# Two transformer blocks on one core: where the pooling chunks, the memory split and the row scaling run in the attention steps

## The reference, cut to what matters

```
h = rmsnorm(x); proj = h @ w_in            # 1024 -> 1888 columns, split in: conv pair, MLA q/kv/rope, diff q/k/v, pool
ya = silu(layernorm(causal_dwconv(a * sigmoid(g)))) @ pw + pw_b       # 31 taps, 256 channels
yb = mla(...)                              # 4 heads, causal softmax over 512 keys
yc = diff_attention(...)                   # 4 heads, two softmax maps each: p = a0 - lam * a1
yd = multiscale_pool(ud)                   # window means of 2, 4, 8, 16 tokens minus the token, times pool_w, pool_scale
x += concat(ya, yb, yc, yd) @ w_out
x += memory_cross_attention(rmsnorm(x), mem)   # k = m @ wk, v = m @ wv, 256 memory tokens
x += conv_glu_ffn(rmsnorm(x))              # 1024 -> 5632 -> 2816 -> 1024
```

## Time and profile before

| | |
|---|---|
| median of 3 runs | 1760.46 us (1758.02 to 1761.1) |
| profiled execution | 1760.47 us, span 1758.6 us |
| busy, share of the span | PE 93%, PE weight load 71%, DVE 63%, ACT 40%, POOL 18% |
| mean granted TensorE clock | 0.962 of full speed |
| scores of step 0, layer 0 and layer 1 | at 196.62 and 1019.22 us |
| end of the last step's work, layer 0 and layer 1 | at about 393.1 and 1214.1 us |

### The profile page before, as it was taken

One profiled execution on the slowest core, in us unless ns is written; L12 is line 12 of the kernel. 1 busy time (PEld: TensorE's weight loads), 2 busy tenths in 40 slices (PEclk: granted clock), 3 DMA queues, 4 the chain that ended last, 5 costly groups with the idle time before them and its releaser, 6 DMA issues. The chain is left out here.

```text
span 1758.6 us, 21905 instructions
## 1 busy us (share of the span) xinstructions
PE 1630.3 (93%) x7472; PEld 1253.1 (71%) x7472; DVE 1108.6 (63%) x1592; ACT 698.8 (40%) x1074; POOL 308.2 (18%) x216
## 2 busy tenths in 40 slices
PE   6889979889999999999998988898999999999996
PEld 3567566568767888888876666666877788888874
DVE  8967785655345764764764867665444675575576
ACT  3132345753244432432442243764343442342343
POOL 6510174522002000000020027551101100000002
PEclk9989899999999999999998998999999999999998
DMA  3242122313202232323324212322211222322323
GB/s 134 52 148 84 49 72 96 102 51 100 84 24 84 96 95 96 97 96 96 95 82 138 75 48 61 109 97 72 91 54 60 84 96 96 96 95 96 96 84 107
DMA packets 46206, 153.38 MB, mean 87 GB/s; under 512 B 5808, under 2 KB 6064, under 8 KB 45232
## 3 DMA queue, kind: packets, MB, share of 16 engines
q1 hardware_dynamic: 46128, 152.34, 26.8%
HBM read 144.97 MB, written 7.34 MB: 87 GB/s over the span
## 5 line engine op out<-in xcount | busy, mean ns | idle before, releaser
L695 ACT ACTIVATE wh<-raw 128x1024 fp32r<-128x1024 f32 x246 | 260.4, 1059 | 660.9 <-PE psum L1249 660.9
L1247 PE MATMUL psum<-a_hi,wh 128*128 128x512 f32 x1072 | 426.1, 397 | 7.9 <-DVE wl L937 7.5
L1249 PE MATMUL psum<-a_hi,wl 128*128 128x512 f32 x1072 | 420.0, 392 | 0.0
L1248 PE MATMUL psum<-a_lo,wh 128*128 128x512 f32 x1072 | 420.0, 392 | 0.0
L937 DVE TENSOR_TENSOR wl<-raw,wh 128x1024 fp32r<-128x1024 f32 x234 | 288.6, 1234 | 193.4 <-ACT wh L695 193.2
L1247 PE MATMUL psum<-b_hi,wh 128*128 128x512 f32 x608 | 240.8, 396 | 10.6 <-DVE wl L937 6.1
L1247 PEld LDWEIGHTS psum<-a_hi,wh 128*128 128x128 f32 x1072 | 203.0, 189 | 57.6 <-DVE wl L937 11.5
L1248 PE MATMUL psum<-b_lo,wh 128*128 128x512 f32 x608 | 237.4, 390 | 0.0
L1249 PE MATMUL psum<-b_hi,wl 128*128 128x512 f32 x608 | 237.4, 390 | 0.0
L1248 PEld LDWEIGHTS psum<-a_lo,wh 128*128 128x128 f32 x1072 | 203.2, 190 | 44.9 <-issue 2.9
L1249 PEld LDWEIGHTS psum<-a_hi,wl 128*128 128x128 f32 x1072 | 202.9, 189 | 42.5
(11 more groups left out here) (214 smaller groups left out, 2188.3 us busy)
## 6 DMA issues: line engine op xcount, KB each, us to landing
raw<-in_w_main SPq DMA_DIRECT2D x106, 512.0 KB, 3.5
raw<-in_w_up SPq DMA_DIRECT2D x88, 512.0 KB, 3.5
raw<-in_w_down SPq DMA_DIRECT2D x32, 512.0 KB, 3.5
raw<-in_w_last SPq DMA_DIRECT2D x16, 384.0 KB, 2.9
bias_scratch<-stage SPq DMA_DIRECT2D x64, 64.0 KB, 1.6
bias<-bias_scratch SPq DMA_DIRECT2D x16, 256.0 KB, 3.9
raw<-in_w_first SPq DMA_DIRECT2D x6, 512.0 KB, 3.5
sw<-in_small SPq DMA_DIRECT2D x2, 1152.0 KB, 6.9
```

The source lines that it names most:

```text
L695: act.activation(wh[:, b].rearrange("p k m -> p (k m)")[:, 0:width], raw[:, b, 0:width], ACT.Copy).then_inc(w_hi, 1)
L1247: pe.matmul(out_ap, wh[:, b, k, :], his[:, k, :], start=(begin and i == 0), stop=False)
L1248: pe.matmul(out_ap, wh[:, b, k, :], los[:, k, :], start=False, stop=False)
L1249: last = pe.matmul(out_ap, wl[:, b, k, :], his[:, k, :], start=False, stop=(end and i == len(tiles) - 1))
```

## The change

What it does, by parts:

1. The pool chunks 13 and 14 of w_in are taken right behind chunk 6 (`IN_ORDER`), so the windows on GpSimd are built before the step loop; `pool0`, `pool1` run in steps 1 and 3. Twelve chunks, not eleven, run before the loop.
2. The memory is split tile by tile in step 2, each tile as soon as the last projection chunk has used the tile of x beneath it (`a_used`); memh and meml of a tile lie together over one tile of `a_hi`. The memory chunks start in step 3. `vc` is transposed and evicted in steps 6 and 8, in the other PSUM bank.
3. VectorE scales the rows itself: one `tensor_scalar` (128x512) behind the inverse for an MLA map; for a differential one a `tensor_scalar` on the second map and the existing combination with the inverse of the first. `wgt` and GpSimd's multiplications go.
4. GpSimd makes the lower parts of chunks 15 to 32 (before: 25 to 30).
5. Steps are moved: ln_mean 10 to 11, ln_var 14 to 15, silu 19 to 21, pw 22, 26 to 23, 25, vx 20, 24 to 18, 22; the first pair of each group of four one step later; taps 30 instead of 34 in the loop; the inverses behind the norms no longer free a PSUM bank, ScalarE's root does.

The diff, cut:

```diff
-CHUNK_AT = {**{t: 11 + t for t in range(4)}, **{t: 10 + t for t in range(5, 13)},
-            **{t: N_WV + i for i, t in enumerate((16, 18, 20, 22, 24, 27, 30, 33))}}
-POOL_LO = {15: 25, 17: 26, 19: 27, 21: 28, 23: 29, 26: 30}
+IN_ORDER = [0, 1, 2, 3, 4, 5, 6, 13, 14, 7, 8, 9, 10, 11, 12]
+CHUNK_AT = {t: 12 + i for i, t in enumerate((0, 1, 2, 3, 4, 5, 6, 7, 9, 11, 13, 15, 17, 19, 21, 23, 26, 29, 32))}
+VX_AT = {18: 0, 22: 1, 28: 2, 36: 3}
+POOL_LO = range(N_WK, N_OUT + 2)
+def pair_step(n):
+    return 2 * n + 5 + int(n % 4 == 0)
...
# GpSimd
-                    for u in range(32):
...
-                        pool.tensor_scalar(e, e, rec[:, m:m + 1], None, ALU.mult).then_inc(scaled_in, 1)
-                        if u in (3, 5):
-                            window_sums(u // 2 - 1)
-                        if u in (4, 6):
-                            window_differences(u // 2 - 2)
-                        if u in POOL_LO:
-                            lower(POOL_LO[u])
+                    for i in range(2):
+                        window_sums(i)
+                        window_differences(i)
+                    for n in POOL_LO:
+                        lower(n)
...
# ScalarE
-                        if t == 4:
+                        if t == 2:
                             act.wait_ge(memf_in, 16)
-                            act.wait_ge(g_full, N_WK)
                             for k in range(KT):
+                                if k < KT - 1:
+                                    act.wait_ge(a_used, k + 1)
+                                else:
+                                    act.wait_ge(g_full, N_WK)
                                 act.activation(memh[:, k, :], memf[:, k, :], ACT.Copy,
                                                scale=v("g_mem", k)).then_inc(m_hi, 1)
...
# VectorE
-                    for n in range(11):
+                    for n in range(12):
...
-                            convolve({8: 0, 9: 1, 10: 4}.get(n, 3))
+                            convolve({8: 0, 9: 2, 11: 4}.get(n, 3))
...
+                            dve.wait_ge(rec_in, m + 1)
+                            dve.tensor_scalar(e, e, rec[:, m:m + 1], None, ALU.mult).then_inc(scaled_in, 1)
...
-                            step(dve.scalar_tensor_tensor(wgt[:, u:u + 1], rec[:, k + 1:k + 2], lam[:, 4:5],
-                                                          sums[:, k:k + 1], ALU.mult, ALU.mult))
-                            dve.scalar_tensor_tensor(e0, e1, wgt[:, u:u + 1], e0, ALU.mult, ALU.add).then_inc(p_ready, 1)
-                        if t < 4:
+                            step(dve.tensor_scalar(e1, e1, rec[:, k + 1:k + 2], lam[:, 4:5], ALU.mult, ALU.mult))
+                            dve.scalar_tensor_tensor(e0, e0, rec[:, k:k + 1], e1, ALU.mult,
+                                                     ALU.add).then_inc(scaled_in, 1)
+                        if t < 2:
                             convolve(4)
-                        elif t > 4:
+                        elif t > 2:
                             convolve(3)
...
# TensorE
+                    gemm(11, 1, a_hi, a_lo, free="in")
...
-                        if t == 10:
+                        if t == 11:
                             pe.wait_ge(acc_done, 2)
                             product("ln_mean", (ones, acc[:, 0, :]), (ones, acc[:, 1, :]))
...
-                        if t in (20, 24, 28, 36):
-                            g = {20: 0, 24: 1, 28: 2, 36: 3}[t]
+                        if t in VX_AT:
+                            g = VX_AT[t]
                             pe.wait_ge(g_act, 8 + 2 * g + 2)
```

More of the change, by code:

```diff
@@ L79 @@
 SW_UQ0, SW_UQ1, SW_K, SW_V, SW_PW, SW_POOL, NSW = 0, 512, 1024, 1280, 1536, 2048, 2304
-V_USES = ([("stat_mix", "dve"), ("stat_q", "dve"), ("stat_kv", "dve"), ("kr", "act"), ("uq0", "dve"),
+V_USES = ([("stat_mix", "root"), ("stat_q", "root"), ("stat_kv", "root"), ("kr", "act"), ("uq0", "dve"),
            ("uq1", "dve"), ("uq2", "dve"), ("uq3", "dve")] + [(f"kn{h}", "act") for h in range(4)] +
[L85 to L91, removed]
+          [("vm0", "act"), ("vm1", "act"), ("pool0", "dve"), ("pool1", "dve"), ("vc0", "act"), ("vc1", "act"),
+           ("ln_mean", "dve"), ("mla0", "dve"), ("ln_var", "root"), ("vx0", "act"), ("mla1", "dve"), ("vx1", "act"),
+           ("pw0", "dve"), ("pw1", "dve"), ("diff0", "act"), ("vx2", "act"), ("sub0", "root"), ("diff1", "act"),
+           ("vx3", "act"), ("sub1", "root"), ("stat_xa", "root")] +
+          [(f"xo{i}", "dve") for i in range(8)] + [("stat_ffn", "root")])
+Y_ORDER = {6: "pool0", 7: "pool1", 2: "mla0", 3: "mla1", 0: "pw0", 1: "pw1", 4: "diff0", 5: "diff1"}
 Y_TILES = list(Y_ORDER)
@@ L559, in _ @@
                     sp.dma_start(vec[:], vecs[layer]).then_inc(vec_in, 16)
-                    loads_of(2, 2, w_main, src_base=2)
+                    for n in (2, 3):
+                        load(n, n % 2, w_main[layer, n])
                     sp.dma_start(sw[:], small[layer]).then_inc(sw_in, 16)
                     sp.dma_start(memf[:], mem_norm).then_inc(memf_in, 16)
-                    loads_of(4, 12, w_main, src_base=4)
-                    loads_of(16, 10, w_main, src_base=16)
+                    for n in range(4, N_WK):
+                        load(n, n % 2, w_main[layer, IN_ORDER[n]])
+                    loads_of(N_WK, 10, w_main, src_base=N_WK)
                     def load_bias(u):
@@ L725, in _ @@
                         act.activation(sqx[:, i, :], sqx[:, i, :], ACT.Sigmoid).then_inc(gate_out, 1)
-                    for n in range(3, 11):
+                    for n in range(3, 12):
                         hi(n + 2)
@@ L954, in inverse @@
                         if cols.stop == S:
-                            ins.then_inc(v_dve, 1)
-                            own_v(name)
+                            step(ins)
                     def scaled(n, dst, b=None):
@@ L1234, in _, with gemm @@
                 def _(pe):
-                    def gemm(n, b, his, los, tokens=S, free=None, tiles=range(KT), ready=None, begin=True, end=True):
+                    def gemm(n, b, his, los, tokens=S, free=None, tiles=range(KT), ready=None, begin=True, end=True, used=None):
                         if begin:
@@ L1250, in gemm @@
                                              stop=(end and i == len(tiles) - 1))
+                            if used and i < len(tiles) - 1:
+                                last.then_inc(used, 1)
                         if end:
@@ L1268, in bank @@
                             before, owner = V_USES[V_AT[V_BEFORE[name]]]
-                            pe.wait_ge(v_dve if owner == "dve" else v_act, V_FREED[owner].index(before) + 1)
+                            freed = {"dve": v_dve, "act": v_act, "root": root}[owner]
+                            pe.wait_ge(freed, V_FREED[owner].index(before) + 1)
                         return V[V_BANK[name]]
```

171 lines of the change are left out of this document (75 added, 96 removed).

## The result

The changed kernel takes 1739.68 us (median of 4 runs, 1737.64 to 1742.63) against 1760.59 for the kernel before on the same chip (4 runs, 1758.02 to 1761.1): 0.9885 of it, 95% interval 0.9868 to 0.9903. It is 20.9 us faster; 9.5 were forecast. The direction and the range held, the size did not: it is more than twice the forecast. The changed kernel was timed in the first comparison only; where others are compared with it, it stands at 0.9881, the ratio of its two medians (by the estimate of 0.9885 each such difference shifts by 0.7 us). 0.001 is 1.76 us, and the difference of two ratios is known to about 0.002, some 4 us.

The account below looks back on a forecast made before the run. TensorE was taken as the bound, busy most of the time at partly reduced clock, with VectorE just behind. Layer 0's terms summed to 191.1 against 196.5 us (-5.4), layer 1 -3.8: 1760.5 to 1751 us, range 1728 to 1771.

Parts of the forecast that it names:

- Steps 0 to 2: First three loop steps: three projection chunks, not four, plus pool0's product; 19.5 us per layer forecast.
- the memory split: Step 2 into step 3: only the last tile left at chunk 14's end; gap of 5.18 us becomes 0.8 to 1.2.
- ln_mean to step 16: Loop stretch with chunks 21 to 23, no pool product and no gap; 26.0 us forecast against 31.7 before.
- tail: End of the layer behind step 33: a chain from pair 15 to `b_lo`, unchanged; 18.1 us forecast.
- Steps 17 to 33: Late loop, chunks 24 to 30: 61 us of TensorE work, 13 of waits, 3 for one clock fall; 77 forecast, 77.3 before.
- the wait for `vx0`: Step 18: TensorE waits for ScalarE's eviction of chunk 24, behind exponentials and ln_var's root; 2.2 us.
- Ahead of the loop: Chunk 11 moved here costs 5.5 us; its late lower part and GpSimd's windows beside VectorE's norms add 2.5 (-0.4 to +6.5).
- rival C: Slower: windows before the loop delay chunk 11's lower part, TensorE falls to 1.2 GHz; 9 us per layer, 1769; chance 0.26.
- Steps 3 to ln_mean: VectorE decides: 31 us of own work plus 12 to 13 held up by GpSimd's lower parts; 42.5 forecast, 43.6 before.
- Outside the stretches: Everything but the part from chunk 10 to the layer's end; the change was taken to touch nothing there.
- A: Rival: TensorE decides all through, lower parts hold VectorE up little; 12 us per layer more gained, 1727; chance 0.19.
- B: Rival, no change: ScalarE waits at `vx0` and `vx1` drop the clock twice, late steps 81 us not 77; 1759; chance 0.21.

## Why the forecast was right, and where it was not

The direction was right, and 20.9 us came where 9.5 were forecast. One step of the working failed, one term was mis-sized, and some of the rest agreed by luck.

*Steps 0 to 2, the memory split, ln_mean to step 16, tail.* 19.5, 26.0 and 18.1 were forecast and 19.8, 25.8 and 18.1 measured. The gap of 5.18 became 0.58 (0.8 to 1.2 forecast), and undoing the start tile by tile alone gives back 9.3 us of the 20.9. The 25.8 agree by luck: ln_mean took 3.59 at the lower clock where 1.9 was put down, so the other terms were 1.9 too large.

*Steps 17 to 33.* 77 forecast, 77.0 measured, with the wait for ScalarE's eviction at step 22 (about 4 forecast, 3.76 measured). Two errors cancel inside: the wait for `vx0`, 2.2 forecast, is 0.52, and the clock falls twice, not once as I priced it, the second time behind the 1.16 ahead of the second pw product; with all of it at full clock the same steps take 64.3 us of TensorE instead of 67.4. That work is slower behind a gap of over 2 us was too general: in the earlier trace rows the pair behind 2.21 takes 1.09 and the transposes behind 2.96 take 0.66, both at full clock.

*Ahead of the loop: the step that failed.* "Together between -0.4 and +6.5; I take +2.5" is -1.2 in the trace (4.3 for the whole part, less the 5.5 of chunk 11), outside even its lower bound. The hold-up was there and larger than I had it: TensorE waits 2.69 for chunk 11, the windows' share of it being 1.9 (0.81 without them). The missing term is the clock. I had the 0.76 of this stretch in view and used it only for rival C, to make things worse; I did not ask what the 1.79 of idle had cost behind it, and that it would be parted if a chunk of 24 dense matmuls came before the products. The products behind chunk 11 take 17.6 us where they took 21.7; moving taps in the kernel before takes the same term out by itself (15.9), and a gap of 4.33 in the changed kernel brings it back (9 us). Twice 3.7 us are 7.4 of the 13.6 by which the profiled span is shorter than forecast.

*Steps 3 to ln_mean: a term that was mis-sized.* 42.5 forecast, 40.5 measured, with the mechanism as described: VectorE decides, through GpSimd's subtractions, and TensorE idles 2.47 and 2.63 (2 and 4 forecast). I took 31 of own work and 12 to 13 of hold-up; the runs show 28.75 and 10.2. I had counted six subtractions at 2 to 2.2 each; by the rows of steps 2 to 5 a hold-up lasts up to 2.2, but there are seven, and 10.2 over them is 1.5 each, since some begin while VectorE does something else. Twice 2 us.

*Outside the stretches.* The span lost 2.4 us where I had nothing. 1.6 of it lie in the 77 us behind the tail of layer 0, where the clock was 0.98 and is 1.00. No run here says why. The part behind layer 1's tail, which no edit touches, took 544.4 us in most of these kernels but 542.7 in one and 546.1 in three, so it may be chance.

*The rivals.* A (TensorE decides all through) is wrong: it does so only with the subtractions cut down, and then at 1716.7 us. Of B's two waits the one for `vx1` cost what the forecast had and the one for `vx0` less; the clock fell twice, as B had it, though not behind `vx0`, and the steps still took 77, not 81. C had the right place and the right cause: the windows delay chunk 11's lower part. But TensorE idled ahead of a dense chunk, and the clock stayed up. Where the idle time was gathered ahead of the products, C's fall of the clock came, for 9 us.

*What the parts are worth*, by runs: the early pool chunks, the split memory and the moved steps together bring all of it and more, 0.9821; of the moved steps, silu's place costs 12 us. Row scaling on VectorE costs 12.7 us of that. The lower parts on GpSimd are worth nothing that could be measured, given that scaling; without it they were not tried.

## What to carry to other kernels

Before pricing a shift of idle time on TensorE, look at the granted clock of the sparse work behind it: 1.8 us of idle ahead of single products cost 5.8 here with what followed it, and 2.7 ahead of a dense chunk cost itself alone. It is a risk and not a rule: 2.6 us ahead of ln_mean lowered the clock in one kernel and not in another. A gap that is shut by moving another engine's work can open again at the next consumer, larger; ask first whether that engine's chain gets shorter or is only reordered. Work moved off GpSimd to relieve a chain meets GpSimd's two-input operations on VectorE: change one of the two, time each half alone, and keep what pays.

## What the runs showed of the hardware that I had not expected

- A `tensor_scalar` of VectorE (0.49 us alone) is held up by GpSimd's `tensor_tensor` just as one with two inputs: 2.27 and 2.11 us, ending 0.3 behind it; its mean over 14 was 1148 ns beside 2.4 us subtractions and 487 ns beside ones cut to 16 columns.
- GpSimd's `tensor_scalar` (1.56 us on average in the differential steps, 1.99 beside the taps) costs three taps of VectorE 0.3 us (2.62 for 2.31); GpSimd's `tensor_tensor` costs them 2.2 (4.51).
- Ahead of the loop the clock fell behind gaps of 1.79 and 4.33 us that stood ahead of single products; it held behind one of 2.69 ahead of a chunk, and behind 1.14, 1.03 and 1.18 ahead of products. In the sparse steps of the loop nearly the same gap came with either level: ln_mean took 3.59 us behind 2.63 and 1.98 behind 2.62, a pair 1.98 and 1.09 behind 0.92 in two layers of one execution, and a pw product was slow (3.55) behind 1.16. No run here shows what settles it.
